# Two feature tiles added ahead of one matmul with ones, in every norm of a two-block model

## The reference

```
h = x + gla_mixer(rmsnorm(x))          # gated linear attention, 4 heads with a value width of 512
h = h + (relu(rmsnorm(h) @ up)^2) @ down
x = rmsnorm(h)                         # ends the first block
x = x + mix(rms_norm(x))               # attention, LRU and short-convolution branches, gated
x = x + (relu(rms_norm(x) @ up)^2) @ down
out = rms_norm(x)

rmsnorm(x) = x * rsqrt(mean(x * x over the features) + 1e-6) * g
o = o * rsqrt(mean(o * o over 512) + 1e-6) * o_norm      # in the mixer, for each head
```

## Time and profile before

| | |
|---|---|
| median of three runs | 2674.23 us |
| the profiled execution | 2673.19 us, span 2671.4 us |
| PE busy | 2649.5 us, 99% |
| PEld busy | 2341.6 us, 88% |
| DVE busy | 1784.5 us, 67% |
| ACT busy | 1348.6 us, 50% |
| POOL busy | 73.6 us, 3%, of which L457 62.6 us in 40 instructions |
| mean granted clock of TensorE | 0.998 |
| DMA | 504.45 MB, 189 GB/s in the mean |

### The profile page before, as it was taken

How to read it: one execution, slowest core, us unless ns; L and a number is a source line. 1 busy time by engine, 2 the same in 40 slices (tenths; PEclk the granted TensorE clock), 3 DMA queues, 4 the chain that set the end, 5 groups by cost and what they waited for, 6 DMA issues and landing times.

```text
span 2671.4 us, 43555 instructions
## 1 busy us (share of the span) xinstructions
PE 2649.5 (99%) x15647; PEld 2341.6 (88%) x15647; DVE 1784.5 (67%) x2056; ACT 1348.6 (50%) x1629; POOL 73.6 (3%) x60
## 2 busy tenths in 40 slices
PE   9999999999999999999999999999999999999998
PEld 7888888888888888888888888888888888888887
DVE  6666877666566567766787666666776566665664
ACT  5546555444444445544675555555554444444443
POOL 1000010000000002200000000000100000000000
PEclk9999999999999999999999999999999999999999
DMA  7794666666666666665556665566666666666663
GB/s 210 168 209 131 195 193 193 196 192 193 190 193 195 194 194 190 195 215 166 166 170 201 192 194 189 188 192 202 194 191 189 194 191 197 193 193 195 189 189 134
DMA packets 507186, 504.45 MB, mean 189 GB/s; under 512 B 17843, under 2 KB 505544, under 8 KB 507096
## 3 DMA queue, kind: packets, MB, share of 16 engines
q1 hardware_dynamic: 505820, 501.60, 60.3%
q10 hardware_dynamic: 1276, 1.63, 1.4%
HBM read 499.50 MB, written 3.67 MB: 188 GB/s over the span
## 4 chain that ended last, share of the span: by engine, by line
PE 97%; DVE 2%; ACT 0%; issue 0%; DMA 0%; POOL 0%; SPq 0%; DVEq 0%; POOLq 0%; ACTq 0%
PE acc L508 60%; PE acc L510 30%; PE acc L503 3%; PE acc L505 2%; DVE wsp L1084 0%; DVE lat L1381 0%; PE misc L617 0%; PE misc L632 0%; DMA xtok<-in_x 0%; PE misc L737 0%; ACT wsp L792 0%; PE misc L599 0%; PE misc L586 0%; PE misc L529 0%; PE misc L686 0%
## 5 line engine op out<-in xcount | busy, mean ns | idle before, releaser
L1084 DVE TENSOR_TENSOR wsp<-raw,wsp 128x1024 fp32r<-128x1024 f32 x944 | 1166.3, 1244 | 580.2 <-ACT wsp L792 552.1
L508 PE MATMUL acc<-xs,wsp 128*128 128x512 f32 x4224 | 1446.7, 390 | 1.8 <-DVE wsp L1084 1.8
L792 ACT ACTIVATE wsp<-raw 128x1024 fp32r<-128x1024 f32 x944 | 993.9, 1058 | 689.9 <-PE acc L510 596.4
L510 PE MATMUL acc<-xs,wsp 128*128 128x256 f32 x4224 | 1166.4, 276 | 0.0
L508 PEld LDWEIGHTS acc<-xs,wsp 128*128 128x128 f32 x4224 | 793.5, 188 | 166.7 <-DVE wsp L1084 2.7
L508 PE MATMUL acc<-hs,wsp 128*128 128x512 f32 x2560 | 873.0, 389 | 0.0
L510 PEld LDWEIGHTS acc<-xs,wsp 128*128 128x128 f32 x4224 | 793.6, 188 | 0.4
L510 PE MATMUL acc<-hs,wsp 128*128 128x256 f32 x2560 | 706.6, 276 | 0.0
L508 PEld LDWEIGHTS acc<-hs,wsp 128*128 128x128 f32 x2560 | 480.6, 188 | 99.3
L510 PEld LDWEIGHTS acc<-hs,wsp 128*128 128x128 f32 x2560 | 480.6, 188 | 0.0
L801 ACT ACTIVATE corr<-acc 128x512 f32<-128x512 f32 x247 | 147.6, 597 | 381.3 <-PE acc L510 371.3
(11 more groups left out here) (223 smaller groups left out, 1011.1 us busy)
## 6 DMA issues: line engine op xcount, KB each, us to landing
raw<-in_w_in SPq DMA_DIRECT2D x224, 512.0 KB, 4.3
raw<-in_mlp_w_up SPq DMA_DIRECT2D x128, 512.0 KB, 4.0
raw<-in_mlp_w_down SPq DMA_DIRECT2D x128, 512.0 KB, 4.2
raw<-in_w_mlp_up SPq DMA_DIRECT2D x128, 512.0 KB, 4.0
raw<-in_w_mlp_down SPq DMA_DIRECT2D x128, 512.0 KB, 4.5
raw<-in_gla_w_in SPq DMA_DIRECT2D x96, 512.0 KB, 4.6
raw<-in_gla_w_out SPq DMA_DIRECT2D x32, 512.0 KB, 4.1
raw<-in_w_out SPq DMA_DIRECT2D x32, 512.0 KB, 4.3
```

The source lines that it names most:

```text
L508: pe.matmul(acc[:, g, j], w_part(0, slot)[:, t, cols], x[:, k0 + k], start=start, stop=False, skip_group_check=True)
L510: ins = pe.matmul(acc[:, g, j, 1], w_part(1, slot)[:, t, cols], x[:, k0 + k, 0], start=False, stop=stop, skip_group_check=True)
L792: act.activation(w_part(0, slot), raw[:, slot], ACT.Copy).then_inc(hi_done, 1)
L1084: dve.tensor_tensor(w_part(1, slot), raw[:, slot], w_part(0, slot).bitcast(F32), ALU.subtract).then_inc(lo_done, 1)
```

## The change

Ahead of each matmul with ones the two tiles are added, and one matmul does what two did.

- GpSimd: `ssq` holds one tile for each sum. A step adds the first tile of `sq`, waits for that (`ssq_half`), then adds the second: two instructions of 256 columns for one of 512, and four for two in norm 2. The clearing (L449) is half as wide.
- VectorE, in the o-norms: the addition of 512 columns stays, followed by a wait for it and an addition of 256 columns.
- TensorE: in `norm` one matmul for each sum, in the o-norms one, in the final norm one for each half of the tokens. That is 8 matmuls of 256 columns less (4 + 1 + 2 + 1) and 2 less with two columns. Each kept matmul is as it was.

```diff
-    ssq = at("ssq", [P, 2, 2, T])
+    ssq = at("ssq", [P, 2, T])
@@ gpsimd
+        HALF0 = {1: 0, 2: 8, 3: 24, 4: 32}
                     for k in range(1 + two):
-                        ins = pool.tensor_tensor(ssq[:, k], ssq[:, k], sq[:, k], ALU.add)
+                        pool.tensor_tensor(ssq[:, k], ssq[:, k], sq[:, k, 0], ALU.add).then_inc(ssq_half, 1)
+                    pool.wait_ge(ssq_half, HALF0[norm] + (1 + two) * (i + 1))
+                    for k in range(1 + two):
+                        ins = pool.tensor_tensor(ssq[:, k], ssq[:, k], sq[:, k, 1], ALU.add)
                     ins.then_inc(ssq_done, 1)
@@ tensor, norm
                 for k in range(1 + two):
-                    for j in range(2):
-                        ins = pe.matmul(M[0][:, k], ones[:], ssq[:, k, j], start=(j == 0), stop=(j == 1),
-                                        skip_group_check=True)
+                    ins = pe.matmul(M[0][:, k], ones[:], ssq[:, k], start=True, stop=True, skip_group_check=True)
@@ tensor, o-norm
-                for j in range(2):
-                    ins = pe.matmul(M[0][:, 0], ones[:], osq[:, j], start=(j == 0), stop=(j == 1),
-                                    skip_group_check=True)
-                ins.then_inc(onorm_mm, 1)
+                pe.matmul(M[0][:, 0], ones[:], osq[:, 0], start=True, stop=True,
+                          skip_group_check=True).then_inc(onorm_mm, 1)
@@ tensor, final norm
         for j in range(TT):
-            for k in range(2):
-                ins = pe.matmul(M[0][:, 0, 2 * j:2 * j + 2], ssq[:, 0, k, j * P:(j + 1) * P], ones[:, 0:2], start=(k == 0),
-                                stop=(k == 1), skip_group_check=True)
+            ins = pe.matmul(M[0][:, 0, 2 * j:2 * j + 2], ssq[:, 0, j * P:(j + 1) * P], ones[:, 0:2], start=True, stop=True,
+                            skip_group_check=True)
@@ vector, o-norm
                 dve.wait_ge(o_copied, step - 1)
-                dve.tensor_tensor(osq[:, 0:2], osq[:, 0:2], osq[:, 2:4], ALU.add).then_inc(osum_done, 1)
+                own.done(dve.tensor_tensor(osq[:, 0:2], osq[:, 0:2], osq[:, 2:4], ALU.add))
+                dve.tensor_tensor(osq[:, 0], osq[:, 0], osq[:, 1], ALU.add).then_inc(osum_done, 1)
```

More of the change, by code:

```diff
@@ L232, in build @@
     f_in, f_out = sem("f_in"), sem("f_out")
-    sq_ready, ssq_done, norm_mm = sem("sq_ready"), sem("ssq_done"), sem("norm_mm")
+    sq_ready, ssq_half, ssq_done, norm_mm = sem("sq_ready"), sem("ssq_half"), sem("ssq_done"), sem("norm_mm")
     std_done, rstd_done, ssq_clear = sem("std_done"), sem("rstd_done"), sem("ssq_clear")
```

## The result

The changed kernel takes 2687.28 us in the median of 19 executions (2670.10 to 2688.95), the kernel before 2674.23 us (2672.95 to 2675.88, 19 executions): 1.003 times as long, 95% interval 1.002 to 1.004: a loss of 0.3%, small but outside the noise. I had forecast 2671.4 us and no measurable difference.

A forecast was written before the change was run, and what follows sets the result against it. TensorE, holding 97% of the chain, bounds the kernel. Savings of 1.72 (o-norms) + 0.86 (norms 1 and 3) - 0.37 (norm 2) + 0.56 (final norm) = 2.77 us give 2671.4 us from 2674.23; range 2669.4 to 2673.6.

The forecast's parts named there:

- rival B: Behind norm 1, up to norm 2, TensorE's pairs fall to a beat slower by 0.014 us: 29 us lost, 2700 us; 4%.
- part 1: Four o-norms: one matmul less each, 0.43 us, 1.72 us saved; VectorE's added 0.45 us each costed at nothing.
- VectorE's longer sum: Sign of failure: in the o-norms, VectorE's sum, some 0.45 us longer, delays a split that TensorE wants.
- The argument against B: Pairs from 403.92 us keep 0.34 us behind a dozen breaks, each followed by a spacer matmul the edit leaves alone.
- To norm 1: Stretch with the four o-norms: 1.72 us saved on TensorE.
- Norm 1: One matmul less on TensorE, 0.43 us saved; GpSimd's second half ends about 1.0 us before TensorE comes.
- Norm 2: GpSimd's last half addition ends 1.23 us later, TensorE's four fewer passes save 0.86: net 0.37 us lost.
- Norm 3: Same picture as at norm 1: one matmul less on TensorE, 0.43 us saved, nothing lost.
- The end: Final norm: four passes go, 0.82 us saved, GpSimd's sum takes 0.26 more: net 0.56 us saved.
- The price of GpSimd's half addition: GpSimd's 256-column addition, in no row: 0.69 us, from 0.64 to at most 0.78.
- A: No turns between GpSimd and VectorE: GpSimd's halves run through together and norm 2 gains, 2670.1 us; chance 0.15.
- C: Clock drops as TensorE idles longer at norm 2: some 3 us of gemm at half speed, 2672.9 us; 5%.

The follow-up runs named there:

- a4: The changed kernel's TensorE part alone, GpSimd and VectorE as in the kernel before: 2685.86 us, 6 of 10 executions at 2685.3 to 2688.2.
- d1: The changed kernel with norm 1's matmul with ones issued twice: 2674.49 us, none of 11 executions near 2688 us.
- a2: The kernel before with only the four o-norms changed, the other norms as before: 2672.86 us, none of 10 executions near 2688 us.
- c1: The changed kernel with the fourth o-norm's matmul issued twice: 2672.77 us, none of 11 executions near 2688 us.
- a3: The kernel before with only the five norms over 2048 features changed, the o-norms as before: 2673.21 us, none of 10 executions near 2688 us.
- c3: The kernel before plus one 256-wide VectorE addition ahead of the splits for the block at 271 us, no norm changed: 2675.02 us, none of 11 near 2690.

## Why the prediction was wrong

**The time.** The range of 2669.4 to 2673.6 us holds all but one of the lower group's executions, and the upper group is rival B, which had 4%. Its nature was right: pairs slower, nothing waited for, held for hundreds of microseconds. Its place and price were not: from 271 us and not from norm 1, 0.0067 us a pair and not 0.014, 15.5 us and not 29, and in about half of the executions. The 0.014 set the slow rate of the token-major blocks (0.353) against the fast rate of the others (0.339). In the same trace the token-major blocks run at 0.3433 us from 128 to 161 us, so like for like the difference is 0.010 us; the two rates were there to be read before the change.

**The step that failed is in part 1.** "So I cost it at nothing" rested on the splits queued behind the sum, those for the block that starts at 260.0, and there the cover was real. The block after it was not looked at. What was missed is that removing a matmul between two blocks takes 0.43 us from the time that VectorE has from the end of one block to the start of the next but one: the cover at gr 4 was 0.55 us and became 0.12. The 13 traces with the gap have a cover of 0.10 to 0.12 us there, that of a4 among them, where VectorE's work is as before; the five without it have 0.43 to 0.55. The sign of failure that the prediction named, VectorE's longer sum, is thus not what used up the cover. As a wait this is tiny: 0.07 us, no entry in the list of waits, and even the trace of the upper group lists none there. By the rule that only TensorE's own time counts, it would be free; what it does to the rhythm is not.

**The argument against B failed too.** "The 17 steps from 403.92 lie behind a dozen such breaks" is true, but each of those breaks had four passes or more. Norm 1's new break has two, and with its spacer it leaves the slow beat as it is (both traces of the upper group); with the matmul doubled the upper group is gone (d1).

**The sum for the lower group** held, step by step. I compare the two profiled executions from the last pair ahead of the first o-norm on (up to there TensorE's stream is the same, and took 1.6 us longer in this execution). To norm 1: 1.63 us saved, for 1.72. Norm 1: 0.43, as forecast. Norm 2: 0.40 lost, for 0.37. Norm 3: 0.42 saved, for 0.43. The end: from ScalarE's last copy of a correction to the last matmul 6.72 us before, 6.09 us now, 0.63 saved for 0.56. The price of GpSimd's half addition, in no row of before, was put at 0.69 and is 0.72 to 0.74 us. The median of the lower group, 2672.3 us, is 0.9 us above the forecast; I leave that open, for the single kernels scatter by as much (a2 +0.4, c1 +0.9, a4's lower group +0.6 against their sums, a3 at its sum). One source of scatter is known: the token-major blocks between 128 and 161 us run at either of their rates, which is worth up to 0.9 us.

**Rivals A and C.** The turns between GpSimd and VectorE are as in the earlier trace rows. By the Trainium skill (SBUF — State Buffer, § SBUF: two separate sides) the pair of ports is locked for whole instructions; the rows of norm 2 after the change, each end about 0.6 us after a split and 1.1 us after a piece, agree. The clock stayed: TensorE was idle for 1.57 us in front of norm 2 and was granted 1.00 in it.

```profile
1107.20:1108.60 1.40, 0.00 (x0) 1.00 0.72 238
```

**What stays open.** Why a pair takes 0.0067 us more in the slow beat, why the gap starts it in one execution and not in the next, why a spacer 44 us behind the gap ends it while one at the gap does not, and whether it is the passes of norm 1 or their time that ends it. That c3, a2 and d1 lose the beat up to norm 1 in some executions is argued from their times; no trace caught it.

## What to carry to other kernels

When the bounding engine gives up work between two stages, look not only at what is queued behind the edit, but at the cover of each handover for the next two stages: the saved time is taken from all of them. A stream of matmuls that is busy throughout can still run at two rates, so count matmuls per stretch, or the distance of their starts, before reading "99% busy" as "nothing to lose". And take ten executions before believing one profile: the one here was of the lower group, and showed a span 1.1 us shorter than before.

## What the runs showed that I had not expected

- Two steady rates of the same pairs of matmuls (512 and 256 columns, weights loaded for each) at the same granted clock of 1.00: 0.3400 and 0.3467 us, 590 and 579 matmuls in 100 us. In the token-major blocks the two rates are 0.3433 and 0.3533 us.
- A delay of 0.07 us of one pair is enough to switch from one to the other: 33 of 59 executions lie in the upper group, and in both traces of it the slow rate starts at that pair and holds for 851 us, across the loops of the output projection and of the first MLP and a break of two passes with a spacer. It ended at norm 2's idle time in both.
- The 36 spacers of the kernel before do not pay here: without them it took 2670.87 for 2674.37 us, 0.9988 times as long (0.9979 to 0.9997).
- GpSimd's addition of two FP32 tiles takes 1.27 us for 512 columns and 0.72 to 0.74 for 256 with VectorE silent, so by an estimate, if the rest goes by the columns, about 0.19 us of it is fixed.
